# Order of the up and down products in the feed-forward blocks of a two-model kernel on one core

## What is computed

```python
def _squared_relu_mlp(h, w1, w2):            # w1: 1024 x 4096, w2: 4096 x 1024
    return jnp.square(jax.nn.relu(h @ w1)) @ w2
# x = x + _squared_relu_mlp(_rmsnorm_2(x, norm_ffn_g[i]), ffn_w1[i], ffn_w2[i])
```

## Time and profile before

| | |
|---|---|
| Median of three runs | 1951.16 us (1944.38, 1951.16, 1952.81) |
| The profiled execution | 1951.88 us, of it the span 1950.1 us |
| PE busy | 1781.6 us (91%) |
| DVE busy | 769.1 us (39%) |
| ACT busy | 492.1 us (25%) |
| `f_ring` loads, 2048 KB each | 30, median 8.2 us from issue to landing |
| Feed-forward stage 0, RWKV, feed-forward stage 1 | about 1299 to 1492, 1493 to 1743, 1744 to 1936 us of the span |

### The profile page before, as it was taken

One profiled execution on the slowest core, in us unless ns is written; L12 is line 12 of the kernel. 1 busy time (PEld: TensorE's weight loads), 2 busy tenths in 40 slices (PEclk: granted clock), 3 DMA queues, 4 the chain that ended last, 5 costly groups with the idle time before them and its releaser, 6 DMA issues. The chain is left out here.

```text
span 1950.1 us, 28666 instructions
## 1 busy us (share of the span) xinstructions
PE 1781.6 (91%) x11538; PEld 1113.7 (57%) x11538; DVE 769.1 (39%) x1338; ACT 492.1 (25%) x788; POOL 195.7 (10%) x141
## 2 busy tenths in 40 slices
PE   8998999999999899889899889989997999889996
PEld 6764333333333333333333478879996788848996
DVE  7944211111111101101111466845555673545555
ACT  4623100000000000000000245444441324124542
POOL 4520000000000000000000235320000105000000
PEclk9998999999999999999999989999998999889998
DMA  7366999999999999999999845555423332335520
GB/s 286 130 240 248 405 429 430 429 430 430 430 430 430 430 430 430 429 430 429 430 430 430 341 164 204 192 205 203 176 86 112 117 100 88 103 115 208 203 105 33
DMA packets 104725, 554.21 MB, mean 284 GB/s; under 512 B 17441, under 2 KB 27682, under 8 KB 79218
## 3 DMA queue, kind: packets, MB, share of 16 engines
q1 hardware_dynamic: 104370, 553.25, 70.0%
q10 hardware_dynamic: 288, 0.02, 0.0%
HBM read 551.15 MB, written 2.10 MB: 284 GB/s over the span
## 5 line engine op out<-in xcount | busy, mean ns | idle before, releaser
L1228 PE MATMUL banks<-front,xsT 128*64 128x512 f32 x1360 | 301.9, 594 | 20.5 <-DMA front<-in_w_up 19.8
L1406 DVE TENSOR_SCALAR xT<-banks 128x512 f32<-128x512 f32 x32 | 22.1, 692 | 638.4 <-PE banks L1235 638.4
L1228 PEld LDWEIGHTS banks<-front,xsT 128*64 128x64 f32 x1360 | 95.3, 137 | 220.6 <-issue 178.9
L1266 PE MATMUL banks<-front,hT 128*64 128x512 f32 x704 | 157.6, 601 | 15.1 <-ACT hT L1322 15.1
L1228 PE MATMUL banks<-more_slots,xsT 128*64 128x512 f32 x688 | 152.8, 594 | 8.2 <-DMA more_slots<-in_w_up 8.2
L2172 PE MATMUL banks<-f_xT_hi,f_w_hi 128*128 128x256 f32 x512 | 145.7, 285 | 1.5 <-DVE f_xT_lo L310 1.5
L2172 PE MATMUL banks<-f_xT_lo,f_w_hi 128*128 128x256 f32 x512 | 145.9, 285 | 0.0
L2172 PE MATMUL banks<-f_xT_hi,f_w_lo 128*128 128x256 f32 x512 | 145.7, 285 | 0.0
L1318 ACT ACTIVATE xT<-xT 128x512 f32<-128x512 f32 x32 | 20.1, 629 | 479.0 <-DVE xT L1406 479.0
L1228 PEld LDWEIGHTS banks<-more_slots,xsT 128*64 128x64 f32 x688 | 48.4, 137 | 110.1 <-issue 91.3
L1266 PEld LDWEIGHTS banks<-front,hT 128*64 128x64 f32 x704 | 49.0, 138 | 108.5 <-issue 89.2
(11 more groups left out here) (429 smaller groups left out, 2939.0 us busy)
## 6 DMA issues: line engine op xcount, KB each, us to landing
front<-in_w_up SPq DMA_DIRECT2D x85, 2048.0 KB, 34.9
front<-in_w_down SPq DMA_DIRECT2D x44, 2048.0 KB, 37.3
more_slots<-in_w_up SPq DMA_DIRECT2D x43, 2048.0 KB, 34.8
f_ring<-in_ffn_w SPq DMA_DIRECT2D x30, 2048.0 KB, 8.2
more_slots<-in_w_down SPq DMA_DIRECT2D x20, 2048.0 KB, 39.1
g_ring<-in_sgu_in SPq DMA_DIRECT2D x7, 2048.0 KB, 7.6
m_raw<-in_w_in SPq DMA_DIRECT2D x6, 2048.0 KB, 8.2
g_ring<-in_sgu_out SPq DMA_DIRECT2D x4, 2048.0 KB, 8.0
```

Of the source, the lines that this page charges most:

```text
L1228: ins = nc.tensor.matmul(c.banks[CAP * h:CAP * (h + 1), bank, :], xsT[:, k, :], up[:, o:o + BANK], start=k == 0, stop=False)
L1266: ins = nc.tensor.matmul(c.banks[CAP * h:CAP * (h + 1), DOWN, :], hT[:, at:at + CAP], down[:, o:o + BANK], start=k == 0, stop=k == KC - 1)
L1406: v.tensor_scalar(glu[:, :], c.banks[:, GLU, :], LIMIT, None, ALU.min).then_inc(glu_ready, 1)
```

## The change

Within each block, `up(2)` is issued ahead of `down(0)`, and `up(3)` ahead of `down(1)`. The products, their operands and all waits inside `up` and `down` stay as they are, as do the programs of the other engines.

```diff
                     up(0)
                     up(1)
+                    up(2)
                     down(0)
-                    up(2)
+                    up(3)
                     down(1)
-                    up(3)
                     down(2)
                     down(3)
```

## The result

The changed kernel takes 1938.83 us, the median of 7 runs (1936.26 to 1939.79), against 1950.42 us of 7 runs before (1944.38 to 1952.81). The ratio is 0.9941, with a 95% interval of 0.9929 to 0.9954: 0.6% faster, 11.6 us between the medians where 10.5 were forecast. Two later sets of runs of the same two kernels gave 0.9953 (0.9936 to 0.9971) and 0.9960 (0.9948 to 0.9973). Over the three sets the gain is 0.4% to 0.6%, 8 to 12 us between the medians.

What follows compares the result with a forecast made beforehand. TensorE bounds the kernel, waiting for h_lo behind VectorE's low parts in both first blocks. Gains of 5.63 + 4.39 + 0.5 = 10.5 us, from 1951.88, give 1941.4 us; own range 1938.5 to 1944.5, full range 1935 to 1948.

Steps and rivals of the forecast that it cites:

- the border of 0.5%: Whole kernel: the full gain, 0.50% below the median, stands at about what a measurement can tell from no change.
- Where the wait is: TensorE before down(0) of each feed-forward stage's first block: 6.5 us waiting for h_lo in two pieces, none in later blocks.
- Stage 0, 5.63 us: First feed-forward stage, first block: 2.87 us from up(2) filling the gap, 2.76 from two products at full clock.
- Stage 1, 4.39 us: Second feed-forward stage, first block: 2.70 us of gap and 1.69 of clock gained, down(0) without a wait.
- its reading of this opening: Second feed-forward stage's opening: after 2.27 us idle, 16 matmuls took 1.94 us, so not at the lower clock level.
- The clock: Products behind both first-block gaps: uncertain term, bounds 0 and 4.45 us, taken as 4.45.
- The rival that the clock would not come back (1945.8): Both first blocks: gaps go but the clock gain fails, 6.1 us gained in all; chance 0.19.
- Transitions, 0.5 us: All 16 blocks: one down product fewer stands behind an up product, 0.03 us each, 0.5 us in all.
- No new wait, and ScalarE's queue with room: Each block: high2(0) done by about 12.6 us, 1.6 us left; rival of ScalarE's queue as bound, 1956.4, chance 0.04.
- The later stage: Rival: the 254 us between feed-forward stages starts earlier, slow stretches fall elsewhere, about 1935 or 1947; chance 0.13.

Runs made afterwards that it cites:

- the second half of the change: Only up(3) moved ahead of down(1), in all blocks, against the kernel before: 1950.21 us, ratio 0.9997.
- the first block alone: New order only in each feed-forward stage's first block, first two blocks written out, against the old order so written out: 1941.16 us, 9.2 us less.
- the filler: Old order, first two blocks written out, plus 12 idle matmuls between up(1) and down(0) of each stage's first block: 1945.40 us against 1950.37.
- the run of the first half: Only up(2) moved ahead of down(0), in all blocks, against the kernel before: 1938.97 us, 12.3 us less.
- the control: Old order with the first two blocks written out ahead of the loop, against the kernel before: 1950.37 us against 1950.14, ratio 1.0007.
- the load: An extra ScalarE copy ahead of each high2 of the loop: old order 1974.14 us against 1948.42 unloaded; new order 1939.24, 1.3 us under the changed kernel.

## Why the prediction was right

The place, the two waits and the end of the slow clock were forecast and came; 1938.83 us lies only 0.3 us inside the own range of 1938.5 to 1944.5. The sum started from the profiled execution, 1951.88 us, which is 1.5 us over the median of seven. The two later sets of the changed kernel, 1940.88 and 1940.51, stand nearer to the 1941.4. Three gains of 0.4% to 0.6% are on the border of 0.5%, as it said.

- *Where the wait is.* Two pieces at the first down product of each stage and nothing in later blocks. Right: the second half of the change, which acts on the later slack, brings nothing (1950.21 against 1951.26), and the first block alone brings 9.2 us.
- *Stage 0, 5.63 us.* Measured 5.53. `up(2)` fills the gap but for 1.29 us (1.30 forecast). The 0.1 us is `down(0)`: it takes 2.89 us, not 2.75. A down product that begins behind a wait is that much longer in the other traces too (2.87 with the filler).
- *Stage 1, 4.39 us.* Measured 4.40, in this execution. In two of the five profiles with the order of the change it is about 1.6 less, since the clock was low for longer at the opening. That the gap here was 2.70 us and not 4.17 the prediction took as it stood. The reason is in the trace of the kernel before: its two up products took 7.30 us in this stage (5.83 in the first), at a clock of 0.77:

```profile
1749.16:1756.46 7.30, 7.30 (x48) 7.26 (x48) 7.30 (x11) 7.27 (x11) 0.00 (x0) 0.77 0.22 61
```

So its reading of this opening, that the clock did not come out low there, holds for the first 16 matmuls alone. That `down(0)` has no wait was luck of this execution; with up products at the full clock, as in the run of the first half, 1.25 us of the gap stay, and the block is as long (28.35 us).
- *The clock.* Of the 10 us, 4.45 were counted on a clock that no longer falls. The filler shows this term alone: 5.0 us between medians, 4.4 or 3.1 in the traces. The mean granted clock of the runs agrees: its median is 0.970 in each of three sets of the kernel before, 0.969 in the control and 0.970 with the second half alone, but 0.972 to 0.974 in the three sets of the changed kernel and 0.9725 with the filler; 4.45 us lost at half clock are 8.9 slow us, by estimate 0.0023 of the mean. The rival that the clock would not come back (1945.8) is refuted for these executions: over `down(0)` the clock is full in each of the profiles of the new order. The rule of the Trainium skill that spoke against it ("TensorE: Matmul & The Clock Gate", section "What's actually happening": the schedule on which the clock is judged does not restart with the kernel) is borne out in part. The slow matmuls do move: in the first stage of the kernel before the up products run at the full clock (5.83 us for two) and those behind the gap are slow; in the control's profile some stand in the up products (7.26 us for two, gap 2.56) and some behind the gap (`down(0)` takes 4.44 us), as in the second stage of the kernel before:

```profile
1302.72:1309.98 7.26, 7.26 (x49) 7.22 (x48) 7.26 (x11) 7.23 (x11) 0.00 (x0) 0.78 0.22 67
1312.54:1316.98 4.44, 4.44 (x13) 3.49 (x13) 2.98 (x4) 0.00 (x0) 0.00 (x0) 0.62 1.03 402
```

But in these four profiles the old order pays wherever they fall: its first blocks last 33.90, 33.81, 33.81 and 32.74 us in the first stage and 32.83, 32.80, 32.67 and 32.74 in the second. When the up products are slow, the gap is shorter and hides it, and fewer of the products behind it are slow; when they are fast, the gap is long and more products behind it are slow. All four are executions with a mean clock of 0.969 to 0.971. The kernel before has others too: 14 of its 64 later runs have 0.974 or more and a median of 1944.6 us, and none of them was profiled, so it is open whether they lost the clock in the first blocks. The 7 runs of the changed kernel with 0.974 or more have a median of 1938.5. The 6.1 us between the two are what the rival gave the gaps alone; the rest of the gain goes with the clock.
- *Transitions, 0.5 us.* Too large. Measured 0.14 + 0.05 us for 14 blocks, a later block going from 22.46 to 22.44; 0.03 us a block was a difference of rows rounded to 0.01, taken 16 times.
- *No new wait, and ScalarE's queue with room.* Right, as the load shows. In the new order the copy waits for `down(0)` as foreseen:

```profile
1338.22 1.06 ACT L2214 ACTIVATE f_w_hi<-f_ring 128x1024 fp32r<-128x1024 f32 x1 [1.04 <-PE banks L2182]
1341.02 0.38 ACT L2233 ACTIVATE f_relu<-banks 128x256 f32<-128x256 f32 x1 [1.74 <-PE banks L2172]
```

It starts at 11.66 us of the block and the relu of chunk 3 at 14.46 finds ScalarE idle for 1.74 us.

- *The later stage.* In the one pair of profiles it gave 1.7 us, in other executions nothing or more. In that pair its 1.7 us, and 1.2 us ahead of the first stage, make 13.0 us out of the 10.1 that the change brings; for the medians of the sets the runs don't show how much of the gain lies there.

## What to carry to other kernels

Count the pieces of a wait before its length: 64 chances and 2 pieces mean a start-up cost, and then only the first pass has to be changed. A gap on TensorE's path can cost its length and a slow stretch behind it, in the second stage here 2.7 us of gap and 1.7 of clock, so independent work moved in pays for both; where none is at hand, matmuls without a purpose brought back the second part here. Slack that an order adds in a steady loop is worth nothing until an engine is loaded, and then much: with the one load tried, the new order lost nothing and the old one 26 us.

## What was not expected

Matmuls that do nothing made the kernel 5.0 us faster in the median (1945.40 against 1950.37, 12 runs each). The unchanged kernel scatters widely: 27 runs in one set lie between 1939.78 and 1952.14 us, five of them below 1946, and the lowest is as fast as the changed kernel's median. The five have a mean granted clock of 0.974 to 0.977, the other 22 of 0.967 to 0.974: the scatter goes with the clock. A single pair of runs could have shown any sign.
